# A two-layer decoder trunk in split fp32: more output-projection matmuls between the steps of the last two attention positions

## The reference, cut to what matters

```
def even_mixer(h, w_qkv, w_o, cos, sin):
    q, k, v = split_heads(h, w_qkv, N_HEADS, HEAD_DIM)
    ...
    o = jnp.concatenate([oa, ob], axis=1)
    return merge_heads(o) @ w_o

def odd_mixer(h, w_qkv, w_o):
    q, k, v = split_heads(h, w_qkv, SB_HEADS, SB_HEAD_DIM)
    o = stick_breaking_attention(q * (SB_HEAD_DIM ** -0.5), k, v)
    return merge_heads(o) @ w_o

def reference(...):
    for i in range(DEPTH):
        m = even_mixer(...) if i % 2 == 0 else odd_mixer(...)
        x = layer_norm(DEEPNORM_ALPHA * x + m, ln_mix_g[i], ln_mix_b[i])
        f = conv_ffn(x, w_up[i], conv_w[i], conv_b[i], w_down[i])
        x = layer_norm(DEEPNORM_ALPHA * x + f, ln_ffn_g[i], ln_ffn_b[i])
    return x
```

## Time and profile before

| | |
|---|---|
| Median of 3 runs | 1278.67 us |
| The profiled execution, its own time | 1279.5 us |
| Its span (first to last instruction) | 1277.7 us |
| Mean granted clock of PE | 0.988 |
| PE busy | 1225.5 us, 96% |
| DVE, POOL, ACT busy | 639.3, 548.0, 506.8 us |
| Chain that ended last | PE 57%, issue 23%, POOL 10%, DVE 6%, ACT 3% |

### The profile page before, as it was taken

The page is one execution under the profiler, slowest core; times in us unless marked ns, Lnnn a source line. Parts: engine busy times, 40 slices in busy tenths (PEclk is TensorE's granted clock), DMA queues, the critical chain, the costliest instruction groups (busy, mean ns, idle before and its releaser), DMA issues.

```text
span 1277.7 us, 17006 instructions
## 1 busy us (share of the span) xinstructions
PE 1225.5 (96%) x6224; PEld 1008.6 (79%) x6224; DVE 639.3 (50%) x1007; ACT 506.8 (40%) x749; POOL 548.0 (43%) x240
## 2 busy tenths in 40 slices
PE   7999998989999999999989999989899999999996
PEld 7877776779888888888778777768888888888885
DVE  2036565285566656522370465553676565552226
ACT  3236465344333333322232456643443333343222
POOL 5535353333444444455434333312364444444551
PEclk9999999989999999999989999999999999999998
DMA  7221222122222222222222111111222222222211
GB/s 287 99 84 58 90 69 81 66 92 107 92 91 88 93 96 98 99 98 98 99 101 100 66 66 66 48 52 66 100 99 98 98 98 98 98 98 99 98 66 66
DMA packets 19879, 117.25 MB, mean 92 GB/s; under 512 B 2433, under 2 KB 2817, under 8 KB 7425
## 3 DMA queue, kind: packets, MB, share of 16 engines
q1 hardware_dynamic: 18256, 112.21, 24.5%
q10 hardware_dynamic: 1584, 4.51, 1.0%
HBM read 110.41 MB, written 2.10 MB: 88 GB/s over the span
## 4 chain that ended last, share of the span: by engine, by line
PE 57%; issue 23%; POOL 10%; DVE 6%; ACT 3%; DMA 0%; POOLq 0%; ACTq 0%; SPq 0%; DVEq 0%
PE bank L829 32%; PE bank L799 18%; POOL w_lo L215 10%; PE bank L875 2%; PE bank L902 1%; PE bank L889 1%; DVE probs L677 1%; PE bank L959 1%; DVE x L572 1%; PE bank L940 1%; PE bank L948 1%; ACT w_hi L267 1%; PE bank L775 1%; DVE x L537 1%; DMA x<-x_in 0%
## 5 line engine op out<-in xcount | busy, mean ns | idle before, releaser
L215 POOL TENSOR_TENSOR w_lo<-w_raw,w_hi 128x1024 fp32r<-128x1024 f32 x196 | 504.3, 2596 | 634.8 <-ACT w_hi L267 577.2
L829 PE MATMUL bank<-xt_hi,w_hi 128*128 128x512 f32 (+1 forms) x1056 | 399.2, 378 | 1.7 <-ACT v_all L304 1.7
L829 PE MATMUL bank<-xt_lo,w_hi 128*128 128x512 f32 (+1 forms) x1056 | 398.8, 378 | 0.0
L829 PE MATMUL bank<-xt_hi,w_lo 128*128 128x512 f32 (+1 forms) x1056 | 394.7, 374 | 0.0
L267 ACT ACTIVATE w_hi<-w_raw 128x2048 fp32r<-128x2048 f32 x94 | 179.6, 1911 | 206.6 <-PE bank L799 206.6
L829 PEld LDWEIGHTS bank<-xt_hi,w_hi 128*128 128x128 f32 x1056 | 201.3, 191 | 38.8 <-ACT v_all L304 2.4
L829 PEld LDWEIGHTS bank<-xt_lo,w_hi 128*128 128x128 f32 x1056 | 201.1, 190 | 38.9 <-issue 4.8
L829 PEld LDWEIGHTS bank<-xt_hi,w_lo 128*128 128x128 f32 x1056 | 201.0, 190 | 33.6
L799 PE MATMUL bank<-w_hi,a_hi 128*128 128x512 f32 x480 | 151.7, 397 | 2.9 <-POOL w_lo L215 1.9
L799 PE MATMUL bank<-w_hi,a_lo 128*128 128x512 f32 x480 | 148.8, 391 | 0.0
L799 PE MATMUL bank<-w_lo,a_hi 128*128 128x512 f32 x480 | 148.6, 391 | 0.0
(11 more groups left out here) (87 smaller groups left out, 1159.5 us busy)
## 6 DMA issues: line engine op xcount, KB each, us to landing
w_raw<-w_stream SPq DMA_DIRECT2D x97, 1024.0 KB, 4.8
x<-x_in SPq DMA_DIRECT2D x4, 512.0 KB, 7.1
gain<-ln_in ACTq DMA_DIRECT2D x4, 512.0 KB, 4.1
shift<-ln_in ACTq DMA_DIRECT2D x4, 512.0 KB, 5.3
qs<-qc SPq DMA_DIRECT2D x16, 128.0 KB, 2.1
ks<-kc SPq DMA_DIRECT2D x16, 128.0 KB, 2.1
out<-x SPq DMA_DIRECT2D x4, 512.0 KB, 2.6
w_raw<-w_stream SPq DMA_DIRECT2D x2, 512.0 KB, 6.0
```

The lines of the kernel that those rows point to most:

```text
L215: pool.tensor_tensor(w_lo[s][:, part], w_raw[s][:, part], w_hi[s][:, part].bitcast(F32), ALU.subtract).then_inc(lo_ready, 1)
L829: mm = pe.matmul(out_bank[:, tok], w, m, start=n == 0, stop=n == len(todo) - 1)
```

## The change

It hands the two last positions more output-projection matmuls. A visit may now name the bank of its tile (`(t, m, g)`: six matmuls into bank 2t + g instead of twelve into two).

- Layer 0: position 6 gets 6 matmuls (tile 0, bank 0, step 0), three before `turn(2)` and three before `turn(3)`. Position 7 gets 30 instead of 24, among them tile 3 in bank 6.
- Layer 1: position 7 gets 48 instead of 24, among them tile 2 in bank 5 and tile 3 in bank 6. Bank 5 is then no longer free for turned probabilities, so position 7 turns all of them through bank 4 (`turn_bank`), and each turn waits for the copy of the one before.
- Bank 6 is written only when `ot_lo` says that position 6's output is out of it.
- Behind position 7 there are 60 (layer 0) and 48 (layer 1) matmuls left instead of 72. They go in another order: both steps for tile 1, both for tile 2, both for tile 3, where before all of step 0 stood ahead of all of step 1.

```
-                for v, (t, m) in enumerate(visits):
+                for v, (t, m, *gs) in enumerate(visits):
+                    gs = gs or (0, 1)
...
-                            for g in range(2):
+                            for g in gs:
...
-                share = (8, 8, 9, 9, 9, 3) if dense else (4, 4, 5, 5, 5, 1)
+                share = (8, 8, 9, 9, 9, 3) if early else (8, 8, 8, 3, 3) if dense else (3, 5, 7, 7, 6)
...
-                share = (10, 11, 14, 9, 2) if dense else (6,) * 4 + (0,)
+                share = (10, 11, 14, 9, 2) if dense else (11, 11, 13, 9, 4)
...
-                    if j >= 2:
+                    if j >= 2 and dense:
                         pe.wait_ge(a["tev_v"] if j % 2 == 0 else a["tev_a"], 2 * i + j // 2)
+                    if j >= 1 and not dense:
+                        pe.wait_ge(a["tev_a"] if j % 2 == 0 else a["tev_v"], 2 * i + (j - 1) // 2 + 1)
...
+                def bank_free(t, n, g):
+
+                    a = A[l]
+                    if (t, g) == (0, 0) and l == 0:
+                        pe.wait_ge(a["q_cp"], NPOS)
+                    if t == 3:
+                        pe.wait_ge(a["ot_lo"], NPOS - 1 + g)
+
+                def outputs(visits, partial):
+                    return row_tiles(out_steps[:2], (a_hi, a_lo), True, False, None, visits, bank_free, partial)
+
+                if l == 0:
+                    beside = [(0, 0, 0)], [(0, 0, 1), (3, 0, 0), (0, 1), (3, 1, 0)]
+                    rest = [(1, 0), (1, 1), (2, 0), (2, 1), (3, 0, 1), (3, 1, 1)]
+                else:
+                    beside = [], [(0, 0), (2, 0, 1), (3, 0, 0), (0, 1), (2, 1, 1), (3, 1, 0)]
+                    rest = [(1, 0), (1, 1), (2, 0, 0), (2, 1, 0), (3, 0, 1), (3, 1, 1)]
...
-                position(b, 6, 0, True)
-
-                out_steps = [(b + AT_O + c, 0, 2 * c) for c in range(N_O)]
-                position(b, 7, 0, False, filler=row_tiles(out_steps[:2], (a_hi, a_lo), True, False,
-                                                             None, [(0, 0), (0, 1)], partial=True))
-
-                pe.wait_ge(A[l]["ot_lo"], 2 * 2)
-
-                def last_output(t, _):
-                    if t == 3:
-                        pe.wait_ge(A[l]["ot_lo"], NPOS)
-                row_steps(out_steps[:2], (a_hi, a_lo), True, False, None,
-                          [(t, n) for n in range(2) for t in (1, 2, 3)], last_output)
+                position(b, 6, 0, True, filler=outputs(beside[0], True))
+                position(b, 7, 0, False, filler=outputs(beside[1], True))
+                for _ in outputs(rest, False):
+                    pass
```

More of the change, by code:

```diff
@@ L150, in build, with turn_bank @@
         block = ctx.enter_context(nc.Block())
+        def turn_bank(j, dense):
+            return 4 + j % 2 if dense else 4
         def filled(c, it):
@@ L304, in values, with turn_out @@
                     act.activation(v_all[:, t, 0:HALF], bank[2 * t][:, :], ACT.Copy).then_inc(V[l]["act"], 1)
-            def turn_out(a, j, g):
+            def turn_out(a, j, g, dense):
                 act.wait_ge(a["t_mm"], g + 1)
                 act.activation(probs_t[0][:, 0:j + 1, j * P:(j + 1) * P],
-                               bank[4 + j % 2][:, 0:(j + 1) * P].rearrange("p (k q) -> p k q", q=P),
+                               bank[turn_bank(j, dense)][:, 0:(j + 1) * P].rearrange("p (k q) -> p k q", q=P),
                                ACT.Copy).then_inc(a["tev_a"], 1)
@@ L387, in odd_body @@
                     if j == 3:
-                        turn_out(a, 1, 4 * i + 1)
+                        turn_out(a, 1, 4 * i + 1, dense)
                         if dense:
@@ L398, in odd_body @@
                 weight_part(3)
-                turn_out(a, 3, 4 * i + 3)
+                turn_out(a, 3, 4 * i + 3, dense)
                 if dense:
@@ L779, in row_tiles @@
             def row_tiles(steps, a, first_chunk, last, rows, visits, before=None, partial=False):
-                for v, (t, m) in enumerate(visits):
+                for v, (t, m, *gs) in enumerate(visits):
+                    gs = gs or (0, 1)
                     if before:
-                        before(t, m)
+                        before(t, m, gs[0])
                     c, it, slot = steps[m]
                     s = c % 2
-                    opens = m not in [n for _, n in visits[:v]]
-                    frees = m not in [n for _, n in visits[v + 1:]] and not partial
+                    opens = m not in [n for _, n, *_ in visits[:v]]
+                    frees = m not in [n for _, n, *_ in visits[v + 1:]] and not partial
                     for u in range(2):
@@ L801, in row_tiles @@
                                                start=first and n == 0, stop=end and n == 2)
-                                if (u, n, g) == (1, 2, 1):
+                                if (u, n, g) == (1, 2, gs[-1]):
                                     if frees:
@@ L856, in project, with even_position @@
                 yield from col_unit(b + AT_QK + c, it, 1, bank[1], None)
-            def even_position(b, c, it, dense, early=False, filler=None):
+            def even_position(b, c, it, dense, early=False, filler=()):
                 a, i = A[0], c + 2 * it
                 par = c % 2
-                more = project(a, 0, b, c + 1, it) if dense else filler
+                more = chain(project(a, 0, b, c + 1, it) if dense else (), filler)
                 if early:
                     more = chain(more, project_early(a, 0, b, c + 2, it))
-                share = (8, 8, 9, 9, 9, 3) if dense else (4, 4, 5, 5, 5, 1)
+                share = (8, 8, 9, 9, 9, 3) if early else (8, 8, 8, 3, 3) if dense else (3, 5, 7, 7, 6)
                 def fill(n):
-                    for _ in range(share[n]):
+                    for _ in range(share[n] if n < len(share) else 0):
                         next(more, None)
@@ L925, in even_position, with odd_position @@
                     pass
-            def odd_position(b, c, it, dense, early=False, filler=None):
+            def odd_position(b, c, it, dense, early=False, filler=()):
                 a, i = A[1], c + 2 * it
                 par = c % 2
-                more = project(a, 1, b, c + 1, it) if dense else filler
+                more = chain(project(a, 1, b, c + 1, it) if dense else (), filler)
                 if early:
                     more = chain(more, project_early(a, 1, b, c + 2, it))
-                share = (10, 11, 14, 9, 2) if dense else (6,) * 4 + (0,)
+                share = (10, 11, 14, 9, 2) if dense else (11, 11, 13, 9, 4)
                 def fill(n):
@@ L944, in turn @@
                     pe.wait_ge(a["p_ok"], 4 * i + j + 1)
-                    if j >= 2:
+                    if j >= 2 and dense:
                         pe.wait_ge(a["tev_v"] if j % 2 == 0 else a["tev_a"], 2 * i + j // 2)
+                    if j >= 1 and not dense:
+                        pe.wait_ge(a["tev_a"] if j % 2 == 0 else a["tev_v"], 2 * i + (j - 1) // 2 + 1)
                     for k in range(j + 1):
-                        mm = pe.transpose(bank[4 + j % 2][:, k * P:(k + 1) * P],
+                        mm = pe.transpose(bank[turn_bank(j, dense)][:, k * P:(k + 1) * P],
                                           probs[0][j % 2][:, k * P:(k + 1) * P], ident[:, :])
@@ L989, in turning, with before @@
                 def turning(i):
-                    def before(t, n):
+                    def before(t, n, g):
                         if t == NT - 1:
@@ L994, in turning, with first_v @@
                     return before
-                def first_v(t, _):
+                def first_v(t, *_):
                     if t == 0:
@@ L1023, in _ @@
                     pass
+                out_steps = [(b + AT_O + c, 0, 2 * c) for c in range(N_O)]
+                def bank_free(t, n, g):
[12 more added lines that the diff above has]
+                    rest = [(1, 0), (1, 1), (2, 0, 0), (2, 1, 0), (3, 0, 1), (3, 1, 1)]
                 position = positions[l]
@@ L1074, in down, with chunk @@
                     turn = turning(2 * l + 2) if last and l < DEPTH - 1 else None
-                    def chunk(t, n):
+                    def chunk(t, n, g):
                         if turn:
-                            turn(t, n)
+                            turn(t, n, g)
                         if first and t == 0:
```

## The result

The changed kernel takes 1282.69 us (median of 22 runs, 1278.91 to 1285.30), the kernel before 1279.21 us in 22 runs beside it (1277.88 to 1280.49). The ratio is 1.0023, 95% interval 1.0016 to 1.0029: 0.23% slower, 3.5 us. The forecast was 1281.6 us with a range of 1279.1 to 1284.2, which was +2.9 us on the 1278.67 us of the three runs it started from; the 22 runs of the kernel before lie 0.5 us above those three.

A forecast was written before the change was run, and what follows sets the result against it. PE, busy 96%, was taken as the bound. Layer 0's +2.15 and layer 1's +0.05 gave +2.2 us; the clock's +0.65 made +2.85, say 2.9, so 1281.6 us, range 1279.1 to 1284.2.

The forecast's parts named there:

- The holes and what fits into them: Positions 6 and 7: fillers fit partly into PE's holes; rest begins 0.81 us later in layer 0, 1.45 in layer 1.
- +0.81 for position 7: Layer 0, position 7: six more matmuls make the rest begin at 234.96 instead of 234.15 us.
- -0.85 where the clock does not fall: Layer 0, position 6: without the half-clock stretch, `weigh(3)` starts up to 0.85 us earlier.
- The single turn bank: Layer 1, position 7: one bank for turned probabilities costs 0; without cover, one copy, 0.55 us.
- The new wait: Third output step, each layer: PE waits 3.45 us for unit 0, 1.0 for unit 1; +4.05 us net.
- The sum without the clock: Both layers, fillers, shorter rest and new waits: +2.15 us in layer 0, +0.05 in layer 1, before the 0.85 gain.
- The clock: Both layers: old half-clock stretches in positions 6 and 7 vanish, falls follow the new waits; together +0.65 us.
- I take 0.6 each, +1.2: Behind each layer's new wait: a clock fall costing 0 to 1.7 us, taken as 0.6 each.
- The hole in position 6: Layer 0: the hole shrinks from 2.54 to 1.8 us, no clock fall after; gain 0 to 0.85, taken as -0.55.
- the clock stays up: Rival 1: same waits for weights, no fall behind them, whole 0.85 gained; +1.35, 1280.0 us; chance 0.27.
- it falls everywhere: Rival 2: clock falls in layer 1's position 7 (+1.3) and behind both new waits (1.0 each); 1284.2 us; chance 0.14.
- the half-speed stretches give back all they took: Rival 3: old slow stretches return -3.4 instead of -0.55, no fall behind new waits; 1277.5 us; chance 0.07.

The follow-up runs named there:

- profiles 2 and 3: Two more profiled executions of the changed kernel, with nothing altered: 1283.74 and 1283.34 us, mean clock 0.987 both.
- the wait filled: Changed kernel plus 14 matmuls by a tile of zeros between the rest and the third output step, both layers: 1279.88 us, ratio 1.0009 to the kernel before.
- step 0 first: Changed kernel with the rest back in the old order, all of output step 0 ahead of step 1: 1272.17 us, ratio 0.9946 to the kernel before.
- bank 6 late: Against step 0 first: layer 1's position 7 makes its two visits into bank 6 at the end of the fillers; 1272.14 us, in a second set 1272.18.

## Why the prediction was right

**The holes and what fits into them: right.** From `turn(3)` of position 6 to the rest of layer 0 it was 21.35 us before (212.80 to 234.15) and is 21.34 after (212.73 to 234.07). The forecast had +0.81 for position 7 and -0.85 where the clock does not fall. In layer 1, from `turn(0)` to the rest, 13.00 us became 14.53: +1.53 against +1.45. The two waits that the fillers brought are where they were put: 0.73 us ahead of layer 0's `turn(0)`, 0.70 us ahead of layer 1's `turn(1)`. The single turn bank costs 0, as said.

**The new wait: right.** The row shows 3.15 and 0.68 us where I had 3.45 and 1.0. (My own terms give 4.77 - 1.36 = 3.41 for the first.) Each is 0.3 us less, mostly because I counted from one start to the next, and the profile counts idle time from a matmul's modelled end. By starts the first matmul of the third step stands 16.94 us behind the beginning of the rest (forecast 17.0), the second unit 2.34 us behind it (2.38). Its whole price, forecast as 4.05 us for each layer, is 3.96 in both. The experiments that undo the order and that make it alone gave 1272.17 for an expected 1272.4, and 1285.05 for an expected 1284.5 to 1286.

**The sum without the clock: right, by 0.1 us.** Forecast 2.15 - 0.85 = +1.30 in layer 0 and +0.05 in layer 1; measured, with no fall in either stretch, +1.15 and +0.08.

**The clock: right in kind, too small.** "I take 0.6 each, +1.2" is the term that was mis-sized. In profiles 2 and 3 the falls cost 0.7 us in layer 0 and 1.8 in layer 1, 2.5 us together. I had bounded one fall at 1.7 us, half of 3.4, and in layer 1 the clock stayed low for 6.8 us. The prediction speaks of two stretches of 3.4 us, but those are only the ones in the last two positions. The profile before has more of them behind its norms, and two of those last 6.8 us, so the longer bound could have been read there. From 277.8 to 284.6 us of its span the mean granted clock is 0.50.

1.2 us without falls and 2.5 us of falls make 3.7 for a measured 3.5. Filling the wait, which took 2.6 to 2.8 us off the median, says the same from the other side. The forecast of 2.9 came as near as it did by some luck: the clock term lacked 1.3 us, and 0.4 of that was made up by two small errors the other way, 0.3 in position 6 (below) and 0.1 in the sum above.

**The hole in position 6: half right.** I expected no fall after it. None of the four profiles of the changed kernel and of the one with the wait filled has one, but with step 0 first and with bank 6 late one of two profiles each does, after the same hole of 1.7 us. Its price is as I had it: with step 0 first the stretch to the norm is 46.26 us with the fall and 45.38 without, 0.88 for a forecast of 0.85. In the changed kernel the whole 0.85 was gained in every profile there is, so the -0.55 was too cautious by 0.3.

**The rivals.** That the clock stays up (1280.0) is what six of 22 runs did by their mean clock, at 1278.9 to 1279.4; only one of them has a profile, and there the change costs 1.2 us as this rival says, while shorter half-clock stretches behind the norms take 1.4 off elsewhere. That it falls everywhere (1284.2) took a fall in layer 1's position 7, and there is none: its hole of 1.39 us is not followed by one in any profile. That the half-speed stretches give back all they took is excluded by the fourth stretch of the table: it is 39.82 and 39.90 us, +0.08 where my sum without this gain has +0.05, though it has a slow stretch in it before and none after.

The Trainium skill, "TensorE: Matmul & The Clock Gate", section "What's actually happening", has activity lift the clock and rest lower it. The wait filled with zeros agrees with it: 14 matmuls that add nothing, no half-clock stretch behind them in the profile, and a median 2.8 us lower. But the profile after has the same 3.15 us of rest and no fall either, so rest of this length does not lower the clock each time.

## What to carry to other kernels

When weights go through a few slots, read the order of the work that uses them from its end: count the matmuls between the last use of a slot and the next need of it, and compare their time with the time of refilling it (here 4.8 us, or 21 matmuls). A reordering that touches no dependency can still put that time on the path, and the profile of before will not show a wait there. And a wait of PE in the middle of dense matmuls can cost more than its length, by a stretch at half clock behind it (here 0.7 and 1.8 us), which one profile may miss: look at the spread of the runs and at their mean clock beside the median.

## What the runs showed of the hardware that was not expected

- The same wait of 3.15 us was followed by a fall of the clock in two profiles of the changed kernel and by none in the third. The length of a wait alone does not decide what the clock does after it, and the runs' times part into two clumps with medians 4.1 us apart (1279.2 and 1283.4).
- In layer 1 the clock then stayed at half for 6.8 us, although PE's rows there show no further wait: it was busy throughout. In layer 0, behind the same wait, it was 3.4 us, in both profiles.
- After a hole of 1.65 to 1.68 us in layer 0's position 6 the clock fell in two of eight profiles; after the old one of 2.5 us it fell in all four that have it.
- Fourteen matmuls by zeros, accumulating into a bank in use, cost 0.1 us where they stood in a wait of 3.15 us, and with them none of 11 runs had a mean clock under 0.991. In 14 of 22 runs without them it was lower.
